# The last 16 steps of the dense expert weights: both keys compared in one VectorE instruction, three of four steps weighed on GpSimd, three buffers in turn

## The reference, cut to what matters

```python
best, pos = lax.top_k(cand, PEER_TOPK)
expert = jnp.take_along_axis(cidx, pos, axis=-1)      # expert = key1 * 128 + key2
gate = jax.nn.softmax(best, axis=-1)
act = jax.nn.gelu(jnp.einsum('td,thkd->thk', xc, u[expert]), approximate=False)
return jnp.einsum('thk,thkd->td', (gate * act), v[expert])
```

## Time and profile before

| | |
|---|---|
| median of 3 runs | 2709.68 us (2708.81 to 2711.16) |
| the profiled execution | 2711.47 us, span 2709.6 us |
| part_dots ends, the 16 steps begin | 2179.13 us |
| last step copied to wmat | 2209.65 us |
| dense product, 128 blocks | 2210.7 to 2689 us |
| last DVE and output work | to 2709.6 us |

### The profile page before, as it was taken

One profiled execution on the slowest core, in us unless ns is written; L12 is line 12 of the kernel. 1 busy time (PEld: TensorE's weight loads), 2 busy tenths in 40 slices (PEclk: granted clock), 3 DMA queues, 4 the chain that ended last, 5 costly groups with the idle time before them and its releaser, 6 DMA issues. The chain is left out here.

```text
span 2709.6 us, 41066 instructions
## 1 busy us (share of the span) xinstructions
PE 2350.5 (87%) x14075; PEld 2090.4 (77%) x14075; DVE 1933.7 (71%) x2948; ACT 1300.3 (48%) x2278; POOL 2053.7 (76%) x1065
## 2 busy tenths in 40 slices
PE   7998999999999999999999887882333469999996
PEld 6997888888888888999988777872322358888885
DVE  4998752633514417456515999989998899999998
ACT  4456455454454454343443012327996844444443
POOL 4887878888888887778783666777788837777773
PEclk9999999999999999999999988985556589999998
DMA  7552555565555554555455999999999969999996
GB/s 233 172 172 94 186 171 185 187 186 186 186 186 186 186 186 161 174 190 168 156 172 177 413 401 386 408 417 422 372 411 401 377 225 386 382 388 375 376 369 262
DMA packets 231588, 722.94 MB, mean 267 GB/s; under 512 B 17389, under 2 KB 53797, under 8 KB 198305
## 3 DMA queue, kind: packets, MB, share of 16 engines
q1 hardware_dynamic: 168416, 356.03, 39.0%
q0 software_dynamic: 57344, 360.74, 33.1%
q10 hardware_dynamic: 5696, 4.47, 0.5%
HBM read 717.51 MB, written 3.67 MB: 266 GB/s over the span
## 5 line engine op out<-in xcount | busy, mean ns | idle before, releaser
L476 POOL TENSOR_TENSOR w_lo<-raw,w_hi 128x1024 fp32r<-128x1024 f32 x464 | 1130.6, 2459 | 258.4 <-ACT w_hi L1223 256.5
L1223 ACT CAST w_hi<-raw 128x1024 fp32r<-128x1024 f32 x464 | 483.9, 1050 | 624.7 <-PE bank L642 412.3
L640 PE MATMUL bank<-B,w_hi 128*128 128x512 f32 x1280 | 455.7, 401 | 15.6 <-DVE B L1823 9.7
L640 PE MATMUL bank<-A,w_hi 128*128 128x512 f32 x1280 | 453.1, 399 | 3.5 <-DVE X L1959 2.1
L642 PE MATMUL bank<-B,w_lo 128*128 128x256 f32 x1280 | 360.6, 282 | 0.0
L642 PE MATMUL bank<-A,w_lo 128*128 128x256 f32 x1280 | 359.4, 281 | 0.0
L1968 DVE TENSOR_TENSOR sq<-bank,T 128x256 f32<-128x256 f32 x128 | 54.2, 424 | 413.0 <-ACT T L1419 412.7
L645 PE MATMUL bank<-A,w_hi 128*128 128x256 f32 x1152 | 330.2, 287 | 7.6 <-POOL w_lo L476 3.4
L594 POOL DMA_INDIRECT vrows<-in_peer_v,ering x192 | 262.8, 1369 | 85.3 <-DVE rest L2383 43.6
L646 PE MATMUL bank<-A,w_hi 128*128 128x256 f32 x1152 | 326.6, 284 | 0.0
L647 PE MATMUL bank<-A,w_lo 128*128 128x256 f32 x1152 | 326.5, 283 | 0.0
(11 more groups left out here) (357 smaller groups left out, 5233.4 us busy)
## 6 DMA issues: line engine op xcount, KB each, us to landing
raw<-in_mlp_w SPq DMA_DIRECT2D x128, 1024.0 KB, 5.1
v_raw<-in_peer_v SPq DMA_DIRECT2D x128, 672.0 KB, 7.4
raw<-in_w_in SPq DMA_DIRECT2D x40, 1024.0 KB, 5.0
raw<-in_cc_w_in SPq DMA_DIRECT2D x64, 512.0 KB, 4.6
raw<-in_cc_w_out SPq DMA_DIRECT2D x16, 1024.0 KB, 5.1
raw<-in_w_out SPq DMA_DIRECT2D x16, 1024.0 KB, 5.1
raw<-in_peer_wq SPq DMA_DIRECT2D x8, 1024.0 KB, 10.9
wq_t<-in_peer_wq SPq DMA_DIRECT2D x2, 2048.0 KB, 24.3
```

The lines of the kernel that those rows point to most:

```text
L476: nc.gpsimd.tensor_tensor(w_lo[:, s % 4], raw[:, s // 2, 2 * (s % 2):2 * (s % 2) + 2, :], w_hi[:, s % 4].bitcast(F32), ALU.subtract).then_ ...
L640: nc.tensor.matmul(bank[m][:].rearrange("p (s t) -> p s t", s=2), wh, both[:, :, kt, :], start=(kt == 0), stop=False)
L1223: nc.scalar.copy(w_hi[:, s % 4], raw[:, s // 2, 2 * (s % 2):2 * (s % 2) + 2, :]).then_inc(hi_done, 1)
```

## The change

DVE's steps 48 to 63 are written out one by one instead of in hardware loops. The steps with q mod 4 = 3 (51, 55, 59, 63; `own_weights`) are made as before: one compare and four `tensor_scalar`. In the other 12 DVE makes both one-hots in one `tensor_tensor` of 2 x 4 x 128 columns, and POOL multiplies the first key's half by the weights in place (`weigh_quad`, 4 x 128 columns, the weight broadcast along 128). PE waits for POOL's multiply (`weighed_ok`) or for DVE (`hot_ok`). A third buffer `hot_more` joins, in the memory of slot 4 of `v_raw`; so SP loads `v_raw` 4 only when all steps are copied out. The waits follow: DVE waits for PE's step q - 3, the weights of part 3 are waited for only by steps that use them, and `part_coefficients(3)` stands behind step 48 instead of 49. POOL's order: the multiplies of steps 48 to 50, then the indices and the first two gathers, then the multiplies of 52 to 62, then gathers 2 to 5, then as before.

```diff
@@ -256,6 +256,8 @@
         hot = at("hot", o_z, [P, 2, 2, 4, KEYS])
         v_bytes = DENSE * 4
         o_v = o_z + 64 * KB - (V_SLOTS + 1) * v_bytes
+        hot_more = at("hot_more", o_v + (V_SLOTS - 1) * v_bytes, [P, 2, 4, KEYS])
+        late_hot = (hot[:, 0], hot[:, 1], hot_more[:])
         v_hi = (at("v_hi0", o_v + V_SLOTS * v_bytes, [P, DENSE], F32R), at("v_hi1", o_z, [P, DENSE], F32R))
         g_lo = at("g_lo", o_z + v_bytes, [P, 2, NT, P], F32R)
         assert v_bytes + 2 * KB <= 8 * KB
@@ -329,6 +331,7 @@
         alpha_ps, rest_ok, mixed_ok = sems("alpha_ps", "rest_ok", "mixed_ok")
         gb_in, var_ok, rt_ok, y_ok, y_out = sems("gb_in", "var_ok", "rt_ok", "y_ok", "y_out")
 
+        hot_ok, HOT_OK, weighed_ok, WEIGHED_OK = xsc_ok, 4, x_ok, 8
         wq_t_in, wq_z_in = poolw_in, wt_in
         gain_in, GAIN_IN = gb_in, 32
         turned_ps, turned_ok, pe_dot_ps, pe_dot_ok = cst2_in, brow_out, rows_in, consts_in
@@ -339,6 +342,18 @@
         def pe_dot(n):
 
             return (bank[2], misc[1], misc[2], misc[3])[(n - len(PE_ROWS)) % 4][:, 0:P]
+
+        def own_weights(q):
+
+            return q % 4 == 3
+
+        def hot_made(q):
+
+            return HOT_OK + sum(5 if own_weights(p) else 1 for p in range(EARLY_STEPS, q + 1))
+
+        def hot_weighed(q):
+
+            return WEIGHED_OK + sum(not own_weights(p) for p in range(EARLY_STEPS, q + 1))
 
         class Steps:
 
@@ -453,6 +468,8 @@
             value_rows(0, 0)
             sp.wait_ge(row_used, RING + NT * SLOTS)
             for i in range(1, V_SLOTS):
+                if i == V_SLOTS - 1:
+                    sp.wait_ge(mat_ok, 2 + 2 * SLOTS // 4)
                 value_rows(i, i)
             for i in range(V_SLOTS, KEYS):
                 if i == KEYS - 8:
@@ -601,10 +618,24 @@
                                       ).then_inc(vring_ok, 1)
                 pool.wait_ge(vring_ok, Q + 1)
 
+            def weigh_quad(q):
+
+                first = 4 * (q - 32)
+                pool.wait_ge(coefT_ok, 2 + (q - 32) // 8)
+                pool.wait_ge(hot_ok, hot_made(q))
+                keys = late_hot[(q - EARLY_STEPS) % 3][:, 0]
+                nc.gpsimd.tensor_tensor(keys, keys, coefT[:, 1, first:first + 4].unsqueeze(2).broadcast_to([P, 4, KEYS]),
+                                        ALU.mult).then_inc(weighed_ok, 1)
+
             V_FIRST = NT * SLOTS // RING
-            pool.wait_ge(row_used, RING + NT * SLOTS)
-            value_experts(0, 0, 0)
-            value_rows(V_FIRST, 0, 0, V_ROWS)
+            for q in range(EARLY_STEPS, 64):
+                if not own_weights(q):
+                    weigh_quad(q)
+                elif q == EARLY_STEPS + 3:
+                    pool.wait_ge(row_used, RING + NT * SLOTS)
+                    value_experts(0, 0, 0)
+                    value_rows(V_FIRST, 0, 0, 2)
+            value_rows(V_FIRST, 0, 2, V_ROWS - 2)
 
 
             pool.wait_ge(mat_ok, 2 + 2 * SLOTS // 4)
@@ -1112,15 +1143,25 @@
                 with pe.Fori(first, first + rounds) as r:
                     for h in range(2):
                         q = 2 * r + h
-                        if 2 * first < EARLY_STEPS:
-                            pe.wait_ge(oh_ok, 13 * q + 13)
-                        else:
-                            pe.wait_ge(oh_ok, 5 * q + (8 * EARLY_STEPS + 5))
+                        pe.wait_ge(oh_ok, 13 * q + 13)
                         pe.wait_ge(mat_ok, q + 1)
                         for i in range(4):
                             last = nc.tensor.matmul(misc[2 + h][:, i * P:(i + 1) * P], hot[:, h, 1, i, :],
                                                     hot[:, h, 0, i, :], start=True, stop=True)
                         last.then_inc(quad_ps, 1)
+
+            def late_quad(q):
+
+                if own_weights(q):
+                    pe.wait_ge(hot_ok, hot_made(q))
+                else:
+                    pe.wait_ge(weighed_ok, hot_weighed(q))
+                pe.wait_ge(mat_ok, q + 1)
+                keys = late_hot[(q - EARLY_STEPS) % 3]
+                for i in range(4):
+                    last = nc.tensor.matmul(misc[2 + q % 2][:, i * P:(i + 1) * P], keys[:, 1, i, :], keys[:, 0, i, :],
+                                            start=True, stop=True)
+                last.then_inc(quad_ps, 1)
 
             def row_turned(n):
 
@@ -1177,10 +1218,12 @@
                 quads(16 + 4 * q, 4)
             part_weights(2)
             pe.wait_ge(coefT_ok, PARTS)
-            quads(24, 1)
+            for q in range(EARLY_STEPS, EARLY_STEPS + 2):
+                late_quad(q)
             part_weights(3)
             pe.wait_ge(coefT_ok, 1 + PARTS)
-            quads(25, 7)
+            for q in range(EARLY_STEPS + 2, 64):
+                late_quad(q)
             pe.wait_ge(mat_ok, 2 + 2 * SLOTS // 4)
             nc.tensor.transpose(misc[3][:, 0:P], coefT[:, 1, :], ident).then_inc(coefT_ps, 1)
 
@@ -2336,19 +2379,23 @@
                 step(of_members(256))
                 dve.sem_inc(half_ok, 1)
 
-            def one_hots(r):
-
-                for h in range(2):
-                    q = 2 * r + (h + 32)
-                    dve.wait_ge(quad_ps, q + 1)
-                    V.tensor_tensor(hot[:, h, 1], iota.unsqueeze(1).broadcast_to([P, 4, KEYS]),
-                                    keyT[:, 1, bass.ds(8 * r + 4 * h, 4)].unsqueeze(2)
-                                    .broadcast_to([P, 4, KEYS]), ALU.is_equal).then_inc(oh_ok, 1)
-                    for i in range(4):
-                        V.tensor_scalar(hot[:, h, 0, i, :], iota,
-                                        keyT[:, 0, bass.ds(8 * r + (4 * h + i), 1)],
-                                        coefT[:, 1, bass.ds(8 * r + (4 * h + i), 1)],
-                                        ALU.is_equal, ALU.mult).then_inc(oh_ok, 1)
+            def one_hots(q):
+
+                first, keys = 4 * (q - 32), late_hot[(q - EARLY_STEPS) % 3]
+                if q != EARLY_STEPS + 2:
+                    dve.wait_ge(quad_ps, 2 + max(EARLY_STEPS, q - 2))
+                if not own_weights(q):
+                    V.tensor_tensor(keys, iota.unsqueeze(1).unsqueeze(1).broadcast_to([P, 2, 4, KEYS]),
+                                    keyT[:, :, first:first + 4].unsqueeze(3).broadcast_to([P, 2, 4, KEYS]),
+                                    ALU.is_equal).then_inc(hot_ok, 1)
+                    return
+                V.tensor_tensor(keys[:, 1], iota.unsqueeze(1).broadcast_to([P, 4, KEYS]),
+                                keyT[:, 1, first:first + 4].unsqueeze(2).broadcast_to([P, 4, KEYS]),
+                                ALU.is_equal).then_inc(hot_ok, 1)
+                dve.wait_ge(coefT_ok, 2 + (q - 32) // 8)
+                for i in range(4):
+                    V.tensor_scalar(keys[:, 0, i, :], iota, keyT[:, 0, first + i:first + i + 1],
+                                    coefT[:, 1, first + i:first + i + 1], ALU.is_equal, ALU.mult).then_inc(hot_ok, 1)
 
             def coefficients(t, n):
                 dve.wait_ge(gelu_ok, t + 1)
@@ -2431,15 +2478,10 @@
             value_low(0)
             part_dots(3, SHARE - 2, 2)
             dve.wait_ge(keyT_ok, 1)
-            dve.wait_ge(coefT_ok, PARTS)
-            with dve.Fori(EARLY_STEPS // 2 - 16, EARLY_STEPS // 2 - 15) as r:
-                one_hots(r)
+            one_hots(EARLY_STEPS)
             part_coefficients(3)
-            with dve.Fori(EARLY_STEPS // 2 - 15, EARLY_STEPS // 2 - 12) as r:
-                one_hots(r)
-            dve.wait_ge(coefT_ok, 1 + PARTS)
-            with dve.Fori(EARLY_STEPS // 2 - 12, 16) as r:
-                one_hots(r)
+            for q in range(EARLY_STEPS + 1, 64):
+                one_hots(q)
             dve.wait_ge(rest_ok, 1)
             dve.wait_ge(coef_ok, 2 + PARTS)
```

## The result

The changed kernel is slower by about what was forecast: 2715.28 us median against 2706.92 of the kernel before in the same comparison (10 executions each), ratio 1.0029 with a 95% interval of 1.0016 to 1.0042. On 2706.92 that is +7.9 us (4.3 to 11.4); forecast were +8.3 against 2709.68. Twelve later executions of it gave 1.0019 (1.0003 to 1.0034).

A forecast was written before the change was run, and what follows sets the result against it. PE bounds the dense product, so DVE's pace of 1.63 us a step in the 16 steps before it counts. Terms +7.1, +0.2 and +0.8 sum to 8.1, for a median of 2718 us; 8 in 10 range 2707 to 2725.

The forecast's parts named there:

- The exclusion: Steps 48 to 63: DVE and POOL instructions on SBUF each wait for the other's whole instruction; +7.1 us.
- The rivals without it: Steps 48 to 63: small instructions free of exclusion, 2714 us, chance 0.12; or no exclusion at all, 2706, chance 0.14.
- no exclusion: Steps 48 to 63: neither engine holds the SBUF path; -3.8 us with the later start, total 2706, chance 0.14.
- M: Length from the first compare to the end of the last copy to wmat; 30.52 us before, forecast +7.3.
- The price of a step: A step handed to POOL costs 2.22 us of DVE's time against 1.63; with twelve such steps +7.1 us.
- The start: First of the 16 steps: one DVE idle gap of about 1.7 us against 1.51 before; +0.2 us.
- The tail: From DVE's end over PE and ACT to the last copy: 2.5 us as before, ±0.
- The rest: From the last copy to wmat to the end of the span: +0.8 us (0 to 3) for late rows.
- late rows: First blocks of the dense product: gathered rows arrive late and DVE waits; +0.8 us (0 to 3).
- the low clock at the start of the dense product: Rival: PE begins the dense product at 1.2 GHz; some 2 us more, 2720; within the forecast's joint chance of 0.68.

The follow-up runs named there:

- e2: Changed kernel with VectorE reading iota from PSUM instead of SBUF; first compare to last copy 26.83 us, ratio 1.0014 to the kernel before.
- the repeat: The changed kernel profiled and timed once more, unaltered; first compare to last copy 35.82 us, ratio 1.0019 to the kernel before.
- e1: Changed kernel with all 16 steps made by VectorE alone, gathers early again; first compare to last copy 28.70 us, ratio 0.9991 to the kernel before.
- the pair of repeats: Changed kernel and kernel before, each run once more unaltered; ratios 1.0019 and 0.9986 to the kernel before.
- e5: As e2, with gathers in pairs at steps 51, 55 and 59; first compare to last copy 28.81 us, ratio 0.9995 to the kernel before.
- e12: e5 run again, unaltered; first compare to last copy 28.61 us, ratio 1.0002 to the kernel before.

## Why the prediction was right, point by point

**The exclusion** was the step on which all hung, and it held, in both directions and for the small instructions. e2 shows it by moving one operand and nothing else. The rivals without it, in whole or in part, fell: with no exclusion M is 26.83. That the prediction put this case at 26.7 (30.52 - 3.8) is in part luck, since it gave the third buffer nothing and priced the small instructions as they run from SBUF.

**The price of a step** was mis-sized in one term. I took 1.28 for POOL's multiply from rows with two full inputs; it took 1.03. With 1.03 - 0.20 in place of 1.28 - 0.20 twelve steps cost 3.0 less, and DVE's work with the start ends 28.0 + 7.3 - 3.0 = 32.3 us after the first compare. Measured were 32.25, and 33.15 in the repeat. That agreement flatters the bookkeeping: I had DVE pay for the multiplies inside its own instructions, but they were stretched by only 3.9, while POOL's waited 6.4 and DVE then stood idle for 7.4 before a free buffer.

**The start.** The lone gap of 1.7 became several, 1.11, 0.63, 2.45, 0.17 and 3.06. The third buffer and the new order of waits, which I gave nothing, are worth 1.8 us of M when DVE works alone (e1); in the changed kernel they can't be seen.

**The tail** I had at 2.5 and unchanged. It was 4.0 in the first profile, where PE ran its last steps partly at the low clock, and 2.7 in the repeat, where it ran them at the full one.

**M in all**: forecast +7.3, measured +5.7 in both pairs of profiles (36.23 - 30.52, 35.82 - 30.13).

**The rest**: forecast +0.8 (0 to 3) for late rows, measured +3.8 and +4.2. This is the other term that was off, in the other direction, and its mechanism isn't shown. Some 0.5 of the 3.8 is the low clock at the start of the dense product; in the pair of repeats both kernels have it. I had it as a rival of +2 that adds to the forecast; it costs a quarter of that, and nothing shows it to come from the change. For the remaining 3 to 4 late rows are the candidate: in the 475 us behind the last copy DVE waits 6.7 and 6.4 us for gathered rows, against 3.6 and 0.8 before. But they are not late where I had looked. I expected the wait in the first blocks, and in the first 60 us DVE waited for none in the first profile and 0.4 us in the repeat; so as I told it, that step failed. And a kernel's rest differs by up to 3.2 us from one profile to the next (e5, e12), so the size of this term is uncertain by nearly as much.

The two errors nearly cancel: M is 1.6 less than forecast, the rest some 3 more. By the profiles the sum is 5.7 + about 4 = 9.7; the medians say 7.9 and the forecast was 8.3. The direction follows from the mechanism; that the total came within half a microsecond is luck.

## What to carry to other kernels

Before moving elementwise work from VectorE to GpSimd, look in the trace for a place where both already compute, and see whether their instructions end behind each other; if so the sum of both counts, however idle GpSimd looks in the windows. If VectorE's instruction has two SBUF operands and one is a constant, try it in PSUM: here it turned 36.2 us into 26.8 with the same sharing. It isn't free for short instructions: four of 128 columns took 1.36 us from PSUM and 1.10 from SBUF. And weigh the stake first: this stretch is 30 us of 2707, so even the best version can't be told from the kernel before.

## What the runs showed of the hardware

GpSimd's 128x512 fp32 multiply with an operand broadcast along the innermost 128 took 1.03 us, against 1.29 for an addition of two full operands of that shape. Whether the repeated operand or the operation makes the difference, no run shows. VectorE's compare of 1024 columns took the same 1.22 us from PSUM as from SBUF. TensorE fell to the lower of its two levels (1.2 GHz) after waiting 2.89 us in a stretch where it had been busy for about two thirds of the time. At the start of the dense product it fell in one profile of the kernel before and stayed at 2.4 GHz in the other, after the same waits of 1.3 and 0.7 us: a low clock in one profile isn't yet a consequence of the change that was made.
